# Sample requests in a decode step: 32-row key scores in turns, and values as the moving operand with a product that picks the heads

## The chip, the cores and the metric

The kernel runs on one core of a Trainium2 chip. The metric is device time in microseconds (us): the kernel before takes 3451.75 us, the median of three runs (3449.54 to 3457.61). Engines are named as in the profile: PE does the matmuls, PEld its weight loads, DVE, ACT and POOL the elementwise work, SP issues transfers.

## The reference, cut to what matters

The program is one layer of a hybrid model, for a prompt of 256 tokens and for 8 sample requests of 4 new tokens each. Two of its branches read caches for the sample requests:

```
def diff_attention(q, k, v, ...):          # 8 heads, two key maps each of 64 columns; 256 cached + 4 new keys
    s = einsum('bqhd,bkhd->bhqk', q, k) * 64**-0.5 + bias          # masked where the key is later
    p = softmax(s);  a = p[:, :, 0] - lam * p[:, :, 1]             # map 0 minus lambda times map 1
    o = einsum('bhqk,bkhe->bqhe', a, v)                            # head width 128
def mem_attention(q, mk, mv):              # 4 heads of 128, 256 memory tokens
    p = softmax(einsum('bqhd,bkhd->bhqk', q, mk) * 128**-0.5)
    o = einsum('bhqk,bkhd->bqhd', p, mv)
```

Everything is float32. After the branches come up-projections, an output projection and a large key-retrieval layer (PEER), which the change does not touch.

## The kernel before

The layer runs in stages, each an explicit block in which every engine has its own program, held together by semaphores. At a block's end the engines meet. The order of the work is the order in which it is written; there is no scheduler. The stages that matter are `diff_sample` and `mem_sample`, each after its prompt counterpart, and `diff_norm` behind them.

Beside the attention stages runs a second stream, `GateStream`: the gate columns of the input projection, cut into ticks. A tick is 24 fp32r matmuls on PE (L974, L975, L977), with splits of the weights on ACT (L916) and POOL (L960), a load on SP (L909) and, every fourth tick, an eviction on ACT (L922). Each attention stage calls `gates.pe(pe, n)` between its own steps, so that PE has n ticks of work while the other engines do softmax or evictions. `TICKS_DIFF_SAMPLE = (3, 3)` and `TICKS_MEM_SAMPLE = (4, 2)` are the ticks ahead of the turn of the probabilities and ahead of the value product.

**diff_sample** goes over 4 pairs of requests. `scores(i)`, for each of the two requests s of a pair: 16 transposes turn the keys (L1410), ACT (L1319) and DVE (L1354) copy them out of four banks, then for each of 8 heads a 256-column matmul against the cached keys (L1421) and a 32-column one against the new keys (L1422) add into 64 rows of bank 4 (8 heads, 2 maps, 4 tokens). The stationary operand is a block of queries that is zero outside its own head's rows, so the 8 heads accumulate into one group of rows. `attend(i)`: three ticks, three transposes of the probabilities, three ticks, then the values: for each request, head and page the values are the stationary operand (128x128) and the probabilities move, 4 columns (L1442, 32 matmuls); 8 more matmuls take the new tokens (L1447). ACT evicts the result (L1330) and then takes the exponentials of the next pair (L1324). PE's program is scores(0), scores(1), attend(0), scores(2), attend(1), scores(3), attend(2), attend(3).

**mem_sample** does the same for 2 groups of 4 requests: 8 transposes (L1683), one eviction by ACT of 1024 columns (L1620), and 4 score matmuls into 32 rows (L1691) for each request; values with 32 matmuls of 4 columns (L1709) for each group.

A float32 matmul (other than a transpose) has two records in the trace, each with its own weight load.

Of the kernel before, what the change touches and what calls it, by code (L numbers as in the profile page):

```python
# [252 lines left out]
def decoder_step_kernel(nc, A, O):  # L253
    top = ExitStack()
    with top:
# [20 lines left out]
        with ExitStack() as left, ExitStack() as right:  # L276
# [5 lines left out]
            with ExitStack() as during_attention:  # L282
                x_high, x_low = (tensor(during_attention, "right", f"x_{part}", [P, KT, T], F32R) for part in ("high", "low"))
                input_projections(nc, G, Z, x_high, x_low)
                signals.restart(130)
                attention(nc, G, Z, ODM, x_high, x_low)
# [25 lines left out]
def constants(const):  # L312
# [59 lines left out]
    C["map_is_0_1"] = const("c_map_is_0_1", np.stack([rm == 0, rm == 1], 1))  # L372
    C["iota"] = const("c_iota", np.broadcast_to(np.arange(P), (P, P)))
# [877 lines left out]
def diff_sample(nc, G, Z, OD, v_new, bias_new, bias_own, row_weights, KP, VP, gates):  # L1251
# [4 lines left out]
    PS, ident, A = (G[k] for k in ("PS", "ident", "A"))  # L1256
    ROWS = DIFF_HEADS * 2 * DEC_SEQ
    FT = DIFF_HEADS
    with ExitStack() as ctx:
# [3 lines left out]
        QB = st.sb("q_blocks", [P, 2, FT * (ROWS + 8)])  # L1263
        S, E, PN = (st.sb(w, [P, PAST + NEW]) for w in ("scores", "exps", "probs"))
        AT, ATN = st.sb("a_T", [P, 2, ROWS]), st.sb("a_T_new", [NEW, ROWS])
        mx, nmx, sums, rec, coef = (st.sb(w, [P, 1]) for w in ("max", "neg_max", "sums", "reciprocal", "coefficient"))
        (pages_loaded, zeroed, k_turned, kT_act, kT_dve, q_ready, scores_done, biased, soft, exps, probs, p_turned,
         aT_ready, o_done, o_ready) = st.sems(
            "pages_loaded", "zeroed", "k_turned", "kT_act", "kT_dve", "q_ready", "scores_done", "biased", "soft", "exps",
            "probs", "p_turned", "aT_ready", "o_done", "o_ready")  # L1270
# [12 lines left out]
        with nc.Block() as block:  # L1283
            @block.sync
            def _(sp):
                sp.dma_start(pages[:], A["page_table"].rearrange("(o b) g -> o (b g)", o=1)).then_inc(pages_loaded, 16)
                sp.wait_ge(pages_loaded, after(16))
# [25 lines left out]
            def _(act):  # L1313
                def turn_keys(i):
                    for s in range(2):
                        act.wait_ge(scores_done, after(i * 2 + s))
# [4 lines left out]
                def attend(i, more=True):  # L1321
# [3 lines left out]
                    if more:  # L1325
# [4 lines left out]
                    act.activation(OD[:, 0:FT, ds(i * 8 + SEQ, 8)].rearrange("p h (b s) -> p h b s", b=2),  # L1330
                                   PS[:, 5, 384:384 + ROWS].rearrange("p (b h s) -> p h b s", b=2, s=DEC_SEQ), ACT.Copy).then_inc(o_ready, 1)
# [11 lines left out]
            def _(dve):  # L1343
                def queries_and_keys(i):
                    for s in range(2):
                        dve.wait_ge(scores_done, after(i * 2 + s))
# [9 lines left out]
                def attend(i, more=True):  # L1356
                    dve.wait_ge(scores_done, after(i * 2 + 2))
# [23 lines left out]
                    dve.wait_ge(aT_ready, after(i * 4 + 1))  # L1381
                    dve.tensor_tensor(at, at, turned[:, :, :, 1, :], ALU.add).then_inc(aT_ready, 1)
                    turned = PS[0:NEW, 5, 2 * P:3 * P].rearrange("p (x m s) -> p x m s", m=2, s=DEC_SEQ)
                    at = ATN[:].rearrange("p (x s) -> p x s", s=DEC_SEQ)
                    dve.tensor_copy(at, turned[:, :, 0, :]).then_inc(aT_ready, 1)
                    dve.wait_ge(aT_ready, after(i * 4 + 3))
                    dve.tensor_tensor(at, at, turned[:, :, 1, :], ALU.add).then_inc(aT_ready, 1)
# [6 lines left out]
                attend(DEC_BATCH // 2 - 1, False)  # L1394

            @block.tensor
            def _(pe):
                def scores(i):
                    for s in range(2):
# [14 lines left out]
                        pe.wait_ge(q_ready, after(i * 4 + 2 * s + 2))  # L1414
                        pe.wait_ge(kT_act, after(i * 4 + 2 * s + 2))
                        pe.wait_ge(kT_dve, after(i * 4 + 2 * s + 2))
                        pe.wait_ge(biased, after(i * 2))
                        rows = slice(s * ROWS, (s + 1) * ROWS)
                        for f in range(FT):
                            q = QB[:, s, f * ROWS:(f + 1) * ROWS]  # L1420
                            pe.matmul(PS[rows, 4, 0:PAST], q, KTT[:, s, f, :], start=(f == 0), stop=(f == FT - 1), skip_group_check=True)  # L1421
                            last = pe.matmul(PS[rows, 4, PAST:PAST + NEW], q, Z[:, DK + f, SEQ:T], start=False, stop=(f == FT - 1),  # L1422
                                             skip_group_check=True)
                        last.then_inc(scores_done, 1)

                def attend(i):
                    gates.pe(pe, TICKS_DIFF_SAMPLE[0])
                    pe.wait_ge(probs, after(i + 1))
                    pe.wait_ge(aT_ready, after(i * 4))
# [3 lines left out]
                    gates.pe(pe, TICKS_DIFF_SAMPLE[1])  # L1433
                    pe.wait_ge(aT_ready, after(i * 4 + 4))
                    pe.wait_ge(o_ready, after(i))
                    for s in range(2):
                        pe.wait_ge(v_loaded[s], after(i * 32 + 32))
                        for h in range(FT):
                            c = slice(s * ROWS // 2 + h * DEC_SEQ, s * ROWS // 2 + (h + 1) * DEC_SEQ)
                            out = PS[:, 5, 384 + c.start:384 + c.stop]  # L1440
                            for g in range(N_PAGES):
                                pe.matmul(out, VP[:, s, g, h * P:(h + 1) * P], AT[:, g, c], start=(s == 0 and h == 0 and g == 0),  # L1442
                                          stop=False, skip_group_check=True)
                    for h in range(FT):
                        out = PS[:, 5, 384:384 + ROWS].rearrange("p (b c) -> p b c", b=2)[:, :, h * DEC_SEQ:(h + 1) * DEC_SEQ]
                        new = ATN[:].rearrange("p (b c) -> p b c", b=2)[:, :, h * DEC_SEQ:(h + 1) * DEC_SEQ]
# [1388 lines left out]
```

## Time and profile before

| | |
|---|---|
| median of 3 runs | 3451.75 us (3449.54 to 3457.61) |
| the profiled execution, span | 3452.9 us; the profile gives no other time for it |
| mean granted TensorE clock | 0.940 |
| `diff_sample`, from PE's first transpose to its last matmul | 1019.97 to 1226.24 us |
| `mem_sample`, the same | 1332.97 to 1425.49 us |
| `diff_norm`, PE's part | 1427.25 to 1433.94 us |

How to read it: times in rows count from the span's start. A row of the timeline is a run of like instructions with its start, its length from first start to last end (the last end is modelled), and in brackets the idle time ahead of it with what ended it. PEclk is the granted clock, 1.00 for 2.4 GHz and 0.50 for 1.2 GHz; in between, a stretch held both. PE's records overlap, so the mean duration of one is longer than its share of the time; lengths of runs, and distances between starts, are what counts.

### The profile page before, as it was taken

To read this page: it belongs to the slowest core of one execution; us is meant where nothing else is said; L and a number is where in the kernel's file an instruction comes from. 1 tells how busy PE (TensorE), PEld (TensorE's weight loads), DVE (VectorE), ACT (ScalarE), POOL (GpSimd) and SP (SyncE) were. 2 spreads that over 40 slices of the span, in tenths; PEclk is the share of its full clock that TensorE was granted. 3 is DMA by queue.
4 is the path that set the end of the run, shared out by engine and by line. 5 is a ranking of instruction groups with operands and counts; after the bars stand their busy time and mean duration, and the time that the engine had idled before them with its cause. 6 is when DMAs were issued, how large, how long until landed. Compare 5 with 4: busy or idle time off the path is not lost. (4 is left out here: it accounts for less than half of the span.)

```text
span 3452.9 us, 52978 instructions
## 1 busy us (share of the span) xinstructions
PE 3186.9 (92%) x21228; PEld 2960.5 (86%) x21228; DVE 1822.6 (53%) x2518; ACT 1254.8 (36%) x1374; POOL 1016.1 (29%) x551
## 2 busy tenths in 40 slices
PE   7999997995879978589989999999999999999998
PEld 6999997774878976589989999999999888888886
DVE  5344443332221000246454889987888467777664
ACT  5323232112432223344332444345555333333332
POOL 0000000002543334200240788887777401111000
PEclk9999998666999879789989999999999999999999
DMA  6554453224454453166676778999999978888764
GB/s 211 174 168 157 161 170 117 88 91 142 143 174 152 133 175 114 42 201 209 205 170 123 200 190 243 230 253 285 279 274 275 347 276 294 318 299 312 288 232 158
DMA packets 446570, 696.71 MB, mean 202 GB/s; under 512 B 30205, under 2 KB 342813, under 8 KB 418878
## 3 DMA queue, kind: packets, MB, share of 16 engines
q1 hardware_dynamic: 397086, 554.35, 51.4%
q10 hardware_dynamic: 40128, 73.42, 7.6%
q0 software_dynamic: 9216, 67.11, 5.1%
q8 instruction: 83, 1.36, 0.2%
q14 instruction: 57, 0.47, 0.0%
HBM read 627.94 MB, written 63.70 MB: 200 GB/s over the span
## 5 line engine op out<-in xcount | busy, mean ns | idle before, releaser
L2455 POOL TENSOR_TENSOR peer_uT_low<-peer_uT,peer_uT_high 128x1024 fp32r<-128x1024 f32 x256 | 615.3, 2427 | 262.1 <-ACT peer_uT_high L2482 261.6
L960 POOL TENSOR_TENSOR gate_low<-gate_raw,gate_high 128x512 fp32r<-128x512 f32 x192 | 244.7, 1299 | 1169.0 <-ACT gate_high L916 1168.9
L2355 PE MATMUL banks<-x_high,peer_uT_high 128*128 128x256 f32 x2048 | 495.5, 284 | 8.8 <-ACT peer_picks_T L2514 7.8
L2356 PE MATMUL banks<-x_low,peer_uT_high 128*128 128x256 f32 x2048 | 490.9, 281 | 0.0
L2355 PEld LDWEIGHTS banks<-x_high,peer_uT_high 128*128 128x128 f32 x2048 | 388.1, 189 | 10.0 <-ACT peer_uT_high L2482 7.0
L2356 PEld LDWEIGHTS banks<-x_low,peer_uT_high 128*128 128x128 f32 x2048 | 387.3, 189 | 0.0
L228 PE MATMUL banks<-x_high,win_high 128*128 128x288 f32 (+1 forms) x1312 | 349.1, 296 | 0.0
L229 PE MATMUL banks<-x_low,win_high 128*128 128x288 f32 (+1 forms) x1312 | 348.7, 295 | 0.0
L2482 ACT ACTIVATE peer_uT_high<-peer_uT 128x1024 fp32r<-128x1024 f32 x256 | 261.5, 1054 | 97.0 <-DVE peer_uT L2605 96.0
L198 ACT ACTIVATE win_high<-win_raw 128x2048 fp32r<-128x2048 f32 x84 | 160.8, 1915 | 334.5 <-DVEq L191 329.2
L2605 DVE STREAM_TRANSPOSE peer_uT<-peer_u 128x1024 f32<-128x1024 f32 x192 | 234.4, 1230 | 81.7 <-DMA peer_u<-in_peer_u_dram 53.2
L2362 PE MATMUL banks<-x_high,peer_uT_low 128*128 128x256 f32 x2048 | 263.8, 282 | 0.0
L204 DVE TENSOR_TENSOR win_low<-win_raw,win_high 128x2048 fp32r<-128x2048 f32 x84 | 192.4, 2291 | 115.8 <-ACT win_high L198 115.8
L2362 PEld LDWEIGHTS banks<-x_high,peer_uT_low 128*128 128x128 f32 x2048 | 250.1, 189 | 0.0
L974 PE MATMUL banks<-x_high,gate_high 128*128 128x288 f32 x768 | 222.6, 311 | 29.1 <-ACT gate_out L922 25.1
L229 PEld LDWEIGHTS banks<-x_low,win_high 128*128 128x128 f32 x1312 | 247.2, 188 | 0.0
L228 PEld LDWEIGHTS banks<-x_high,win_high 128*128 128x128 f32 x1312 | 246.5, 188 | 0.2
L975 PE MATMUL banks<-x_low,gate_high 128*128 128x288 f32 x768 | 217.7, 303 | 0.0
L2422 PE MATMUL banks<-x_high 128*128 128x512 f32 x512 | 201.6, 394 | 12.5 <-DVE x_low L2762 12.5
L2530 ACT ACTIVATE peer_uT_high<-peer_u 128x2048 fp32r<-128x2048 f32 x64 | 122.8, 1919 | 228.6 <-PE banks L2424 201.8
L2530 ACT ACTIVATE x_high<-peer_area 128x2048 fp32r<-128x2048 f32 x64 | 122.7, 1919 | 220.2 <-PE banks L2424 218.1
L2463 POOL DMA_INDIRECT peer_area<-in_peer_v_dram,peer_expert_row x32 | 62.0, 1936 | 473.7 <-DVE peer_area L2730 472.6
(390 smaller groups left out, 6884.3 us busy)
## 6 DMA issues: line engine op xcount, KB each, us to landing
win_raw<-in_w_in_dram SPq DMA_DIRECT2D x38, 2048.0 KB, 8.1
peer_u<-in_peer_v_dram SPq DMA_DIRECT2D x64, 1024.0 KB, 6.4
peer_area<-in_peer_v_dram SPq DMA_DIRECT2D x64, 1024.0 KB, 5.0
gate_raw<-in_w_in_dram SPq DMA_DIRECT2D x96, 512.0 KB, 4.0
peer_u<-in_peer_u_dram SPq DMA_DIRECT2D x192, 256.0 KB
peer_u<-in_peer_u_dram ACTq DMA_DIRECT2D x192, 256.0 KB
w_raw<-in_w_up_ret_dram SPq DMA_DIRECT2D x8, 2048.0 KB, 9.6
w_raw<-in_w_out_dram SPq DMA_DIRECT2D x8, 2048.0 KB, 8.8
```

Source lines behind the costliest of these rows:

```text
L228: pe.matmul(out, w, xh[:, k, :], start=(k == 0), stop=False)
L229: pe.matmul(out, w, xl[:, k, :], start=False, stop=False)
L960: pool.tensor_tensor(self.low[:, p % 2, c, :, :], self.raw[:, p % 4, :, c * P:(c + 1) * P], self.high[:, p % 2, c, :, :], ALU.subtract).th ...
L974: pe.matmul(out, high, self.xh[:, 4 * q + k, :], start=(q == 0 and k == 0), stop=False)
L975: pe.matmul(out, high, self.xl[:, 4 * q + k, :], start=False, stop=False)
L2355: pe.matmul(out, UH[:, c, k, :], XH[:, k, 0:DENSE], start=(k == 0), stop=False)
L2356: pe.matmul(out, UH[:, c, k, :], XL[:, k, 0:DENSE], start=False, stop=False)
L2362: last = pe.matmul(out, UL[:, c, k, :], XH[:, k, 0:DENSE], start=False, stop=(k == KT - 1))
L2455: pool.tensor_tensor(UL[:, m % 2, part, :], UT[:, m % 2, part, :], UH[:, m % 2, part, :], ALU.subtract).then_inc(low, 1)
L2482: act.activation(UH[:, m % 2, part, :], UT[:, m % 2, part, :], ACT.Copy).then_inc(uT_high, 1)
L2530: act.activation(VH[n % 4], V[n % 4], ACT.Copy).then_inc(v_high, 1)
L2605: dve.transpose(UT[:, m % 2, b * HALF:(b + 1) * HALF, :].rearrange("p c (E e) -> p E c e", E=4), u_block(m)[:, :, cols].rearrange("p E (c ...
```

## The change

In `diff_sample` a row group is now 32 rows instead of 64: request s and half of the heads (4 heads, 2 maps, 4 tokens). Both requests' keys are turned first, in one go of 32 transposes. Then four rounds follow; in each, one 256-column matmul for each of the four row groups, then one 32-column matmul for each. The number of score matmuls is as before (16 and 16 for a pair); a stationary operand has 32 columns instead of 64.

For the values the operands change places: 32 columns of the turned probabilities (all heads of one request, one page) are stationary, and the values move, 512 columns at a time, into banks 0 and 1. That is 8 matmuls for a pair, and the four combinations of request and page go to the four row groups. Their result holds all products of probabilities of any head with values of any head. ACT and DVE copy it to `ds_values`, and 8 matmuls with a constant 0/1 matrix `pick` keep what belongs together, sum over the two pages, and turn it: values stationary, 8 columns moving. Of the six ticks, one now stands between the value product and this pick. The new tokens' products are left for the end of the stage, 8 matmuls of 32 columns, added by one DVE instruction. The semaphore signals go from 130 to 140, and two small constants are loaded.

`mem_sample` has the same two edits: transposes of two requests, then their scores in turns; 8 value matmuls of 512 columns over four row groups, accumulating over the two halves of the tokens in one bank, an ACT copy, and 4 pick matmuls of 16 columns.

```diff
-                        rows = slice(s * ROWS, (s + 1) * ROWS)
-                        for f in range(FT):
-                            q = QB[:, s, f * ROWS:(f + 1) * ROWS]
-                            pe.matmul(PS[rows, 4, 0:PAST], q, KTT[:, s, f, :], start=(f == 0), stop=(f == FT - 1), skip_group_check=True)
-                            last = pe.matmul(PS[rows, 4, PAST:PAST + NEW], q, Z[:, DK + f, SEQ:T], start=False, stop=(f == FT - 1),
...
+                    tiles = [(s, half, slice((2 * s + half) * TILE, (2 * s + half + 1) * TILE)) for s in range(2) for half in range(2)]
+                    for r in range(FT // 2):
...
+                        for s, half, rows in tiles:
+                            pe.matmul(PS[rows, 4, 0:PAST], queries(s, half), KTT[:, s, half * (FT // 2) + r, :], start=(r == 0),
...
+                        for s, half, rows in tiles:
+                            last = pe.matmul(PS[rows, 4, PAST:PAST + NEW], queries(s, half), Z[:, DK + half * (FT // 2) + r, SEQ:T],
...
-                    gates.pe(pe, TICKS_DIFF_SAMPLE[1])
-                    pe.wait_ge(aT_ready, after(i * 4 + 4))
+                    gates.pe(pe, TICKS_DIFF_SAMPLE[1] - 1)
+                    pe.wait_ge(aT_ready, after(i * 6 + 2))
...
+                    for w in range(2):
+                        for s in range(2):
                             for g in range(N_PAGES):
-                                pe.matmul(out, VP[:, s, g, h * P:(h + 1) * P], AT[:, g, c], start=(s == 0 and h == 0 and g == 0),
...
+                                j = N_PAGES * s + g
+                                last = pe.matmul(PS[32 * j:32 * j + 32, w, :], AT[:, g, s * ROWS // 2:(s + 1) * ROWS // 2],
+                                                 VP[:, s, g, w * 512:(w + 1) * 512], start=True, stop=True, skip_group_check=True)
+                    last.then_inc(o_done, 1)
+                    gates.pe(pe, 1)
...
+                    pe.wait_ge(values_act, after(i + 1))
+                    pe.wait_ge(values_dve, after(i + 1))
...
                     for h in range(FT):
...
+                        last = pe.matmul(PS[:, 5, 384 + h * 8:384 + h * 8 + 8], O[:, h * P:(h + 1) * P], pick[:, h, :],
+                                         start=True, stop=True, skip_group_check=True)
+                    last.then_inc(picked, 1)
```

On PE, in `diff_sample`, the turn and the scores of the first pair before. `ident` is the identity of the transposes, `ds_k_T` the turned keys, `Z` (L1410) the loaded keys and (L1422) the new ones; the left-out rows alternate in the same way:

```order
L1410 MATMUL banks<-ident,Z 128x128 x16
L1421 MATMUL banks<-ds_k_T,ds_q_blocks 64x256
L1422 MATMUL banks<-Z,ds_q_blocks 64x32
...
L1422 MATMUL banks<-Z,ds_q_blocks 64x32
L1410 MATMUL banks<-ident,Z 128x128 x16
L1421 MATMUL banks<-ds_k_T,ds_q_blocks 64x256
L1422 MATMUL banks<-Z,ds_q_blocks 64x32
```

and after, at the same place:

```order
L1431 MATMUL banks<-ident,Z 128x128 x32
L1446 MATMUL banks<-ds_k_T,ds_q_blocks 32x256 x4
L1449 MATMUL banks<-Z,ds_q_blocks 32x32 x4
L1446 MATMUL banks<-ds_k_T,ds_q_blocks 32x256 x4
L1449 MATMUL banks<-Z,ds_q_blocks 32x32 x4
```

The second request's transposes have moved ahead of the first's scores, and the scores of both stand in one block, four row groups in turn.

On PE, the end of `attend(0)` before; the last gate matmuls, the values of both requests, the new tokens' values and the next pair's transposes:

```order
L977 MATMUL banks<-x_high,gate_low 128x288 x4
L1442 MATMUL banks<-ds_a_T,Z 128x4 [waits signal_179,signal_176,signal_174]
L1442 MATMUL banks<-ds_a_T,Z 128x4 x15
L1442 MATMUL banks<-ds_a_T,Z 128x4 [waits signal_180]
L1442 MATMUL banks<-ds_a_T,Z 128x4 x15
L1447 MATMUL banks<-ds_a_T_new,Z 128x2x4 x8
L1410 MATMUL banks<-ident,Z 128x128 [waits signal_165,signal_177]
```

and after:

```order
L985 MATMUL banks<-x_high,gate_low 128x288 x4
L1469 MATMUL banks<-Z,ds_a_T 32x512 [waits signal_185,signal_184,signal_174]
L1469 MATMUL banks<-Z,ds_a_T 32x512 x7
L982 MATMUL banks<-x_high,gate_high 128x288 [waits signal_132]
...
L985 MATMUL banks<-x_high,gate_low 128x288 x4
L1479 MATMUL banks<-ds_pick,ds_values 128x8 [waits signal_179,signal_174,signal_178,signal_177]
```

The 32 matmuls of 4 columns have become 8 of 512, a tick (signal_132 is its split weights) has moved in behind them, and 8 pick matmuls follow it; the new tokens' 8 are gone from here.

## Rows read from the trace of the kernel before

**Rows 1.** The page: the granted clock in 40 slices of the span.
```profile
PEclk9999998666999879789989999999999999999999
```

**Rows 2.** Windows over the stages: us, busy by engine, PEclk, DMA share, GB/s.
```profile
1019.90:1226.70 206.80, 194.60 (x1292) 179.93 (x1292) 23.82 (x74) 45.36 (x88) 61.18 (x48) 0.85 0.43 144
...
1332.90:1365.40 32.50, 23.44 (x128) 13.23 (x128) 2.41 (x13) 10.28 (x14) 0.67 (x1) 1.00 0.07 20
```

**Rows 3.** Timeline of PE, 1062 to 1092: values, new tokens, keys turned.
```profile
1073.43 9.98 PE L1442 MATMUL banks<-ds_a_T,Z 128*128 128x4 f32 x64
1083.35 3.58 PE L1447 MATMUL banks<-ds_a_T_new,Z 32*128 32x8 f32 x16
1086.86 3.67 PE L1410 MATMUL banks<-ident,Z 128*128 128x128 f32 x16
1091.52 0.62 PE L1421 MATMUL banks<-ds_k_T,ds_q_blocks 128*64 128x256 f32 x2 [0.99 <-DVE ds_k_T L1354]
```

**Rows 4.** Windows over the four value blocks, the first and the sum.
```profile
1073.40:1086.90 13.50, 13.50 (x83) 13.46 (x81) 0.00 (x0) 0.00 (x0) 0.00 (x0) 0.65 0.01 3
...
sum 54.50, PE 54.44 PEld 54.20 DVE 0.00 ACT 0.02 POOL 0.00; mean PE 13.61 PEld 13.55 DVE 0.00 ACT 0.01 POOL 0.00
```

**Rows 5.** Windows over the turns and scores: pair 2, and the sum of four.
```profile
1086.86:1103.42 16.56, 14.59 (x98) 11.39 (x97) 4.07 (x11) 4.16 (x9) 2.49 (x2) 0.87 0.53 174
...
sum 68.21, PE 58.55 PEld 45.10 DVE 16.37 ACT 15.68 POOL 7.48; mean PE 19.52 PEld 15.03 DVE 5.46 ACT 5.23 POOL 2.49
```

**Rows 6.** Timeline, 1019 to 1037: both turns of the first pair, softmax of it.
```profile
1019.97 3.34 PE L1410 MATMUL banks<-ident,Z 128*128 128x128 f32 x16 [9.27 <-DMA Z<-in_cache_diff_k_dram]
...
1028.77 1.97 PE L1410 MATMUL banks<-ident,Z 128*128 128x128 f32 x16
...
1036.39 0.42 DVE L1359 TENSOR_TENSOR ds_scores<-banks,diff_bias_new 128x256 f32<-128x256 f32 x1 [4.93 <-PE banks L1422]
...
1038.97 0.38 DVE L1349 TENSOR_SCALAR ds_q_blocks<-Z 64x32 f32<-64x32 f32 x2
1039.38 1.29 DVE L1354 COPY ds_k_T<-banks 128x512 f32<-128x512 f32 x2
...
1040.92 0.62 PE L1421 MATMUL banks<-ds_k_T,ds_q_blocks 128*64 128x256 f32 x2 [2.67 <-DVE ds_k_T L1354]
```

**Rows 7.** Timeline of PE, 1332 to 1350: `mem_sample`'s turns and scores.
```profile
1332.97 1.06 PE L1683 MATMUL banks<-ident,Z 128*128 128x128 f32 x8 [0.94 <-PEq L1479]
1335.15 1.91 PE L1691 MATMUL banks<-msm_k_T,msm_q_blocks 128*32 128x256 f32 x8 [1.11 <-ACT msm_k_T L1620]
1336.99 1.09 PE L1683 MATMUL banks<-ident,Z 128*128 128x128 f32 x8
```

**Rows 8.** Groups by line and form, 1332.9 to 1434: busy, mean ns of one.
```profile
L1691 PE MATMUL banks<-msm_k_T,msm_q_blocks 128*32 128x256 f32 x64 | 15.3, 382 | 9.0 <-ACT msm_k_T L1620 9.0
...
L1691 PEld LDWEIGHTS banks<-msm_k_T,msm_q_blocks 128*32 128x32 f32 x64 | 6.4, 109 | 16.0 <-ACT msm_k_T L1620 10.9
```

**Rows 9.** Timeline of PE, 1384 to 1434: `mem_sample`'s values, `diff_norm`.
```profile
1386.29 8.92 PE L1709 MATMUL banks<-msm_probs_T,memory_cache_v 128*128 128x4 f32 x64
...
1416.78 8.71 PE L1709 MATMUL banks<-msm_probs_T,Z 128*128 128x4 f32 x64
1427.25 6.69 PE L1755 MATMUL banks<-dn_squares,ones 128*128 128x288 f32 x16 [1.76 <-ACT dn_squares L1741]
```

**Rows 10.** Timeline of PE, 854.9 to 857.2: matmuls over 64 input rows, two halves.
```profile
855.29 1.14 PE L1222 MATMUL banks<-dp_qkv_T 64*128 64x256 f32 x8
```

**Rows 11.** Windows over three ticks at either clock, and over the ticks behind L1709.
```profile
1052.80:1062.60 9.80, 9.80 (x75) 9.78 (x73) 0.00 (x0) 3.16 (x5) 5.74 (x5) 1.00 0.44 133
1189.10:1201.70 12.60, 12.10 (x75) 11.86 (x75) 0.69 (x3) 5.54 (x13) 8.13 (x7) 0.83 0.86 295
...
1395.20:1410.40 15.20, 14.70 (x100) 14.46 (x99) 0.52 (x2) 6.11 (x13) 10.14 (x8) 0.90 0.17 54
```

**Rows 12.** The transfers, 1100 to 1140: busy share in 40 slices of 1 us.
```profile
DMA  0059200000799998999999970000000000000039
```

More of the change, by code:

```diff
@@ L1444, in attend @@
+                    last.then_inc(o_done, 1)
+                    gates.pe(pe, 1)
+                    if i == 0:
+                        pe.wait_ge(pick_loaded, after(16))
+                    pe.wait_ge(values_act, after(i + 1))
+                    pe.wait_ge(values_dve, after(i + 1))
+                    pe.wait_ge(aT_ready, after(i * 6 + 6))
                     for h in range(FT):
[L1445 removed]
@@ L1446, in attend @@
-                        new = ATN[:].rearrange("p (b c) -> p b c", b=2)[:, :, h * DEC_SEQ:(h + 1) * DEC_SEQ]
-                        last = pe.matmul(out, v_new[:, h * P:(h + 1) * P], new, start=False, stop=True, skip_group_check=True)
-                    last.then_inc(o_done, 1)
+                        last = pe.matmul(PS[:, 5, 384 + h * 8:384 + h * 8 + 8], O[:, h * P:(h + 1) * P], pick[:, h, :],
+                                         start=True, stop=True, skip_group_check=True)
+                    last.then_inc(picked, 1)
@@ L1454, in _ @@
                 attend(DEC_BATCH // 2 - 1)
+                for h in range(FT):
+                    last = pe.matmul(PS[:, 4, h * NEW:(h + 1) * NEW], v_new[:, h * P:(h + 1) * P], ATN[:, h, :],
+                                     start=(h == 0), stop=True, skip_group_check=True)
+                last.then_inc(new_done, 1)
 GROUP = 4
@@ L1603, in _ @@
             def _(sp):
+                sp.dma_start(pick[:], C["pick_mem"]).then_inc(pick_loaded, 16)
                 gates.sp(sp, TICKS_MEM_SAMPLE[0])
@@ L1689, in scores @@
                             pe.wait_ge(exps, after(i))
                         for f in range(FT):
-                            last = pe.matmul(PS[b * ROWS:(b + 1) * ROWS, 4, 0:MEM_TOKENS], QB[:, b % 2, f * ROWS:(f + 1) * ROWS],
-                                             KTT[:, b % 2, f, :], start=(f == 0), stop=(f == FT - 1))
-                        last.then_inc(scores_done, 1)
+                            for b in (2 * pair, 2 * pair + 1):
+                                last = pe.matmul(PS[b * ROWS:(b + 1) * ROWS, 4, 0:MEM_TOKENS], QB[:, b % 2, f * ROWS:(f + 1) * ROWS],
+                                                 KTT[:, b % 2, f, :], start=(f == 0), stop=(f == FT - 1), skip_group_check=True)
@@ L1695, in attend @@
+                        last.then_inc(scores_done, 2)
                 def attend(i):
@@ L1698, in attend @@
                     pe.wait_ge(pT_ready, after(i))
+                    pe.wait_ge(o_ready, after(i))
                     for k in range(2):
```

139 lines of the change are left out of this document (86 added, 53 removed).

## The prediction

> **What bounds the kernel now.** I read the granted clock by slices first [rows 1]. The reader is to see that the clock is down in slices 8 to 11 (an earlier stage) and again, at 7 to 8 tenths, in single slices up to 19, each of 86 us, where the attention stages lie, and not in the last half. The windows over the two sample stages come next [rows 2]: in `diff_sample` PE is busy for 194.6 of 206.8 us, at a mean clock of 0.85, while DVE has 23.8 us, ACT 45.4 and POOL 61.2. So PE alone sets the time there, and what PE saves the program saves, as long as nobody is late for it. In `mem_sample`'s score part PE is busy for 23.4 of 32.5 us, and waits for an eviction the rest of the time.
>
> Then the timeline of PE. A value block is 64 records in 9.98 us, the new tokens 16 in 3.58, and the next keys' turn takes 3.67 for 16 transposes [rows 3], where the same 16 take 1.97 elsewhere [rows 6]: the clock is down. The windows over the value blocks say so: the first holds 80 records in 13.5 us at a clock of 0.65, and all four come to 54.5 us [rows 4]. In full-clock time that first block is 13.5 x 0.65 = 8.8 us, or 0.11 us a record. Each block begins at the full clock after ticks and ends at half of it; matmuls of 4 and 8 columns are what PE does before it falls. The turns and scores of the four pairs take 68.2 us [rows 5], with one wait of about 1 us for the last DVE copy at each turn [rows 3] and 2.67 us at pair 1, where the softmax of pair 0 stands ahead of the copies [rows 6]. In `mem_sample` a request is 1.06 us of turning, 1.11 us of wait and eight records in 1.84 us (1335.15 to 1336.99) [rows 7], that is 0.23 us for a record of 256 columns in a 32-column group.
>
> **What the score edit costs and gives.** The number of matmuls stays. A block of one request is (1036.3 - 1028.8 - 2.0 - 1.0) / 8 = 0.57 us a head [rows 3, 6], of which two records of 256 columns are 0.46 and the 32-column ones 0.11. If the four row groups run side by side, a round costs PE what one matmul of each kind costs: 0.57 us, so 2.4 us a pair with the filling, where it was 8.8 to 9.0. If they run one after another, a pair stays at 16 x 0.57 = 9.1.
>
> No row of before has two 32-column groups side by side. What I have is the nearest thing, two halves of the array by input rows [rows 10]: eight records of 256 columns in 1.14 us, last end included, so about 1.0 us, where eight records in one group take 1.84 us [rows 7]. They overlap twofold, although the program gives both matmuls of the first half before those of the second. PE thus starts work for a free part of the array past matmuls that wait for a busy one. I take the row groups as fully side by side, and keep one after another as the other end.
>
> The Trainium skill, TensorEngine Tiling (Array Packing), Key Properties, says that different tiles can load weights and multiply in parallel; with the speedup of 3.07 that TensorE: Matmul & The Clock Gate, Measured speedup vs the span model, gives for four tiles by rows, the fourfold terms would be 1.3 times as long, and my sum some 5 us less. That page also has a rule against this change (The mechanism: weight loads overlap running matmuls only where the row group differs, and all tiles here have the same rows). By it the gain of the turns would go, which is my serial rival below. The trace does not bear it out within one group: in the 128x32 matmuls a weight load of 0.109 us stands between records that are 0.23 us apart.
>
> The waits: both turns now come first. Pair 0: 3.3 us of transposes at half clock, 2.0 for the second request, then DVE's last copy, 0.9, then 2.4: 8.6 us. Pair 1: the scores started 4.63 us after the last ones (1036.29 to 1040.92), and behind the softmax DVE now has two sets of query blocks and copies (0.38 and 1.29) [rows 6] where it had one: 6.4 us, and 2.4. Pairs 2 and 3: the same chain without the 1.2 us of bias and maximum, which DVE does during the tick behind the value product: 5.2 and 2.4. Together 8.6 + 8.8 + 7.6 + 7.6 = 32.6 us against 68.2: **35.6 us** less. ACT's exponential still waits for the end of the pair's last product, so the copies can't start earlier; this is what becomes late next.
>
> **The value edit.** Eight matmuls of 512 columns: a record of twice 256 columns is 2 x 0.23 = 0.46, less the fixed part, 0.44 us. Side by side, two rounds of two records are 1.76 us a pair; one after another 7.0. The pick is 16 records at 0.11: 1.8 us. The copies to `ds_values` (512 columns, 0.60 on ACT by its key copy, 0.65 on DVE, half of two in 1.29 [rows 6]) lie beside the tick that was moved behind the product, 3.27 us (9.8 for three [rows 11]); without that cover they would cost 0.8 us a pair. The tick itself is moved, not added; its loads are issued as before, since SP runs up to four ticks ahead. DVE's extra instructions for the new tokens, two of some 0.2 us, lie beside a tick too. At the end come 16 records for the new tokens, 1.8 us, and one DVE addition, with its wait 0.6 us. Sum: 4 x 3.56 + 2.4 = 16.6 us against 54.5 [rows 4]: **37.9 us** less. About half of it is the clock: 320 records at 0.11 would be 35 us.
>
> Behind the third block three ticks took 12.6 us at a clock of 0.83, against 9.8 at 1.00 [rows 11]. I expect the clock to stay up now, as it did in `mem_sample`'s scores, where turns and waits alternate with 256-column matmuls at 1.00 [rows 2, 7]: **2.8 us** less.
>
> **mem_sample and diff_norm.** Two requests are turned (2.1 us), ACT's second eviction of 1.02 us ends 1.3 us later, and eight matmuls in two groups take 1.9: 5.3 us for two, against 8.1. With 0.4 us for the exponential ahead of group 1's copies: 32.5 - 4 x 5.3 - 0.4 = **10.9 us** less. Values: 8.8 and 8.7 us [rows 9] become 1.76 + 0.9 each: **12.2** less. The four ticks behind the first block, 15.2 us [rows 11], become 13.1: **2.1** less. `diff_norm`'s 16 records took 6.69 us at low clock [rows 9]; at 0.26 us each they are 4.2: **2.5** less.
>
> **Small costs.** The array changes its grouping some 12 times more, at 0.1 us each by the excess of a first record: 1.2 us. Ten more signals, 0.2. The two constants are loaded beside the page table and the first ticks.
>
> **Sum:** 35.6 + 37.9 + 2.8 + 10.9 + 12.2 + 2.1 + 2.5 - 1.4 = 102.6 us less than the profiled execution's span of 3452.9, so 3350.3. The median of the runs is 1.1 us under that span, so I say 3350. Later stages do not depend on when they start.
>
> **Rivals.**
> 1. *Half of the overlap* (3370 us): PE keeps strictly to the program's order, so that the second record of a matmul waits for its first and only neighbours overlap, or the four moving operands share a read path, each being 128 rows deep where the halves of [rows 10] read every row once. A 256-column matmul then costs 0.23 in the scores (4.7 us a pair), a 512-column one 0.44: 9 + 7 + 3.5 = 20 us more. For it: nothing in before reads four streams. Against it: the order in [rows 10].
> 2. *No overlap* (3417 us): scores of 9.1 and values of 7.0 a pair in `diff_sample`, 3.7 and 7.0 in `mem_sample`: 27 + 21 + 7.5 + 10.5 = 66 us more. It would still be 1.0% faster, by fewer waits and by the clock.
> 3. *Slower, 3471 us*: each change of row group empties the array and leaves the weight load uncovered. There are 32 changes a pair in the scores, 8 in the values, 48 in `mem_sample`, 208 in all. The price by a record's latency of 0.38 against its spacing of 0.23, plus a load of 0.11 [rows 7, 8], is 0.26 us, so 54 us on top of rival 2. It turns slower from 0.17 us a change. Against it: the change between the halves in [rows 10] cost nothing.
> 4. *The gain is there, but PE waits or slows* (3366 us): keys arrive late, or the clock falls between pick and scores, where 1.8 us of 8-column matmuls are followed by 5 us of transposes and a wait. SP issues the keys of pair 3 ahead of three gate loads; these transfers start at about 1110, 7 us after `attend(1)` began at 1103.42 [rows 5], and keep the engines busy until 1124 [rows 12]. The whole of `attend` shrinks to 23.8 us (six ticks 19.6, turn 0.6, values and pick 3.6), so a margin of 3 us stays. If the clock falls at three or four turns, each costs 3 to 4 us.
>
> **Chances.** Full overlap 0.55; half of it 0.20; waits or clock 0.08; none 0.13; slower 0.04. The time is that of the first. A range from 3338 to 3405 holds the first, second and fourth with their errors and leaves out most of the two serial ones. A change under 0.2%, 7 us, can't be told from none: faster 0.95, same 0.01, slower 0.04.
>
> **What would show it.** Timeline of PE: a round of four 256-column matmuls about 0.5 us long, four row groups' records starting within some tens of ns; a score block of 2.4 us, a value block of 1.8, a pick of 1.8 at full clock; the wait ahead of the scores 1.3 us in pairs 2 and 3; the clock over `diff_sample` at 0.95 or more, and the stage some 130 us long. I am wrong if a score block is over 4.5 us, if the clock still falls in each pair, or if idle time ahead of a tick grows over 2 us.

## The result and the profile after

| | before | after | predicted |
|---|---|---|---|
| median | 3454.68 us (4 runs, 3449.54 to 3458.73) | 3352.91 us (4 runs, 3349.06 to 3357.17) | 3350 (3338 to 3405) |
| ratio | | 0.9708, 95% interval 0.9691 to 0.9726 | 0.9705 |
| span of the profiled execution | 3452.9 us | 3353.8 us | 3350.3 |
| mean granted clock | 0.940 | 0.947 | |
| PE in `diff_sample`, first transpose to last matmul | 206.3 us | 133.0 us | 130.0 |
| PE in `mem_sample`, the same | 92.5 us | 68.2 us | 67.3 |

The change is faster by 2.9%. Of the 99.1 us between the two spans, 73.3 lie in `diff_sample` and 24.3 in `mem_sample`; the stages between are 1.4 us shorter, `diff_sample` starts 0.8 us earlier, and from `diff_norm` on nothing is gained. (The predicted stage lengths are those of before less the terms of the sum, without its 1.4 us of small costs.)

The page after, granted clock by slices, answers [rows 1]:

```profile
PEclk9999999666999899799989999999999999999999
```

With 84 us a slice, `diff_sample` lies in slices 13 and 14 now (9 and 8 tenths) and `mem_sample` in slice 16 (9); what is left below lies in other stages. The 8 of slice 14 comes from behind the stage: the clock was 1.00 from 1090.0 to the stage's end at 1152.2 us, and 0.50 in the 22 us after it. The windows over `diff_sample`, over `mem_sample`'s turns and scores, and over the ticks behind its first values (us, busy by engine, PEclk, DMA share, GB/s) answer [rows 2, 11]:

```profile
1019.10:1152.40 133.30, 122.27 (x1116) 111.08 (x1116) 27.25 (x87) 47.84 (x92) 61.20 (x48) 0.99 0.67 224
...
1257.40:1277.50 20.10, 15.32 (x129) 10.38 (x129) 2.21 (x13) 9.85 (x14) 0.79 (x1) 1.00 0.12 36
...
1301.00:1314.90 13.90, 13.40 (x100) 13.16 (x100) 0.52 (x2) 6.12 (x13) 10.09 (x8) 1.00 0.20 63
```

The clock over `diff_sample` rose from 0.85 to 0.99. PE's idle time did not go: 11.0 of 133.3 us, where it was 12.2 of 206.8. What went is work of PE and the slow clock.

The timeline of PE from `attend(0)`'s values to pair 2's scores answers [rows 3 to 5]:

```profile
1055.81 1.92 PE L1469 MATMUL banks<-Z,ds_a_T 128*32 128x512 f32 x16
...
1060.97 1.85 PE L1479 MATMUL banks<-ds_pick,ds_values 128*128 128x8 f32 x16
1062.67 2.38 PE L1431 MATMUL banks<-ident,Z 128*128 128x128 f32 x20
1065.45 1.53 PE L1431 MATMUL banks<-ident,Z 128*128 128x128 f32 x12 [0.40 <-DVE ds_k_T L1369]
1067.98 0.64 PE L1446 MATMUL banks<-ds_k_T,ds_q_blocks 128*32 128x256 f32 x8 [1.00 <-DVE ds_k_T L1369]
1068.41 0.24 PE L1449 MATMUL banks<-Z,ds_q_blocks 128*32 128x32 f32 x5
...
1068.51 0.61 PE L1446 MATMUL banks<-ds_k_T,ds_q_blocks 128*32 128x256 f32 x7
...
1069.90 0.27 PE L1449 MATMUL banks<-Z,ds_q_blocks 128*32 128x32 f32 x8
```

Values and pick are 1.92 and 1.85 us for the 13.5 of before. The turn of 32 transposes starts at the full clock and takes 4.31 us with one wait for an eviction. A round of scores is 8 records of 256 columns and 8 of 32, each round begins 0.5 us after the last, and the block ends 2.19 us after it began (1067.98 to 1070.17). From the end of the pick to the scores' end are 7.4 us where [rows 5] has 16.56.

Pair 1's turn, and the groups of the score and value lines over the stage (busy, mean ns of one, idle before):

```profile
1031.05 1.97 PE L1431 MATMUL banks<-ident,Z 128*128 128x128 f32 x16 [3.49 <-DMA Z<-in_cache_diff_k_dram]
1033.45 1.97 PE L1431 MATMUL banks<-ident,Z 128*128 128x128 f32 x16 [0.44 <-DMA Z<-in_cache_diff_k_dram]
```

```profile
L1446 PE MATMUL banks<-ds_k_T,ds_q_blocks 128*32 128x256 f32 x128 | 8.5, 382 | 4.0 <-DVE ds_k_T L1369 4.0
L1469 PE MATMUL banks<-Z,ds_a_T 128*32 128x512 f32 x64 | 7.7, 598 | 0.0
L1479 PE MATMUL banks<-ds_pick,ds_values 128*128 128x8 f32 x64 | 7.4, 251 | 0.0
```

The keys of pair 1 are now late: PE waits 3.9 us for them. And a trap for readers: one score record still lasts 382 ns, as in [rows 8], though 128 of them fill 8.5 us (66 ns each). Records in different row groups overlap, so the mean duration tells nothing of the throughput.

`mem_sample` after, the first turn and scores, the end of the stage, and ACT's last steps, answer [rows 7, 9]:

```profile
1257.47 1.94 PE L1727 MATMUL banks<-ident,Z 128*128 128x128 f32 x16 [1.05 <-PEq L1516]
1260.56 1.92 PE L1736 MATMUL banks<-msm_k_T,msm_q_blocks 128*32 128x256 f32 x16 [1.16 <-ACT msm_k_T L1661]
1262.41 1.97 PE L1727 MATMUL banks<-ident,Z 128*128 128x128 f32 x16
...
1318.29 1.92 PE L1753 MATMUL banks<-Z,msm_probs_T 128*32 128x512 f32 x16
1324.57 1.06 PE L1761 MATMUL banks<-msm_pick,msm_values 128*128 128x16 f32 x8 [0.99 <-ACT msm_values L1676]
1327.92 6.61 PE L1806 MATMUL banks<-dn_squares,ones 128*128 128x288 f32 x16 [2.28 <-ACT dn_squares L1792]
```

```profile
1322.02 0.41 ACT L930 ACTIVATE gate_out<-banks 128x288 f32<-128x288 f32 x1 [5.37 <-PE banks L985]
1323.62 0.41 ACT L930 ACTIVATE gate_out<-banks 128x288 f32<-128x288 f32 x1 [1.19 <-PE banks L985]
1323.93 0.59 ACT L1676 ACTIVATE msm_values<-banks 128x512 f32<-128x512 f32 x1
```

The last copy of the products is not hidden: ACT's program has the eviction of the last gate tile ahead of it, and that waits for the very tick behind the value product (1323.62), so the copy starts when the tick is over. And `diff_norm` is as long as before.

### The profile page after: what moved, and what is told of

The parts are those of the page before. It is cut to its first block and busy times, and to the rows that moved or that the text cites. A ratio compares the mean times of both kernels' runs of the same rounds, so it can differ in the third digit from the quotient of the medians.

```text
span 3353.8 us, 52494 instructions
## 1 busy us (share of the span) xinstructions
PE 3095.2 (92%) x20972; PEld 2873.7 (86%) x20972; DVE 1820.4 (54%) x2531; ACT 1257.0 (37%) x1380; POOL 1016.0 (30%) x551
## 5 line engine op out<-in xcount | busy, mean ns | idle before, releaser
L2533 ACT ACTIVATE peer_uT_high<-peer_uT 128x1024 fp32r<-128x1024 f32 x256 | 260.5, 1055 | 63.3 <-DVE peer_uT L2656 62.6
```

Source lines behind the costliest of these rows:

```text
L2533: act.activation(UH[:, m % 2, part, :], UT[:, m % 2, part, :], ACT.Copy).then_inc(uT_high, 1)
```

## The experiments

All ratios are against the kernel before in the same job. Because executions scatter by some 5 us and `diff_sample` starts up to 10 us apart in them, PE's own time in the two stages (first transpose to last matmul) is the sharper measure; the ratio has the last word where a version as a whole is judged.

| | median us | ratio, 95% | `diff_sample` | `mem_sample` |
|---|---|---|---|---|
| before | | 1 | 206.3 | 92.5 |
| the change | 3352.91 | 0.9708 (0.9691 to 0.9726) | 133.0 | 68.2 |
| 1 scores of `diff_sample` alone | 3422.12 | 0.9908 (0.9873 to 0.9942) | 179.1 | 98.1 |
| 2 values of `diff_sample` alone | 3412.15 | 0.9873 (0.9851 to 0.9894) | 167.0 | 95.7 |
| 3 `mem_sample` alone | 3426.41 | 0.9921 (0.9903 to 0.9939) | 206.8 | 68.1 |
| 4 before, ticks among the values | 3440.39 | 0.9958 (0.9943 to 0.9972) | 197.0 | 92.5 |
| 5 change, group by group | 3374.52 | 0.9769 (0.9747 to 0.9791) | 149.0 | 71.7 |
| 6 change, two groups of 64 rows | 3358.59 | 0.9722 (0.9701 to 0.9743) | 140.3 | 68.2 |
| 7 change, pair 1's keys first | 3354.65 | 0.9701 (0.9682 to 0.9720) | 132.4 | 68.2 |
| 8 as 7, ticks behind the turns | 3346.19 | 0.9688 (0.9670 to 0.9705) | 132.1 | 61.3 |
| 9 change, two rounds a group | 3363.10 | 0.9732 (0.9712 to 0.9752) | 142.2 | 68.2 |
| 10 the change again, with 9 and 11 | 3352.73 | 0.9697 (0.9678 to 0.9715) | 134.2 | 68.2 |
| 11 as 8 again | 3343.51 | 0.9681 (0.9666 to 0.9696) | 131.6 | 62.6 |

**1 to 3: one part alone.** The first takes the new `scores` and keeps the old `attend`, the second the other way round, the third has the old `diff_sample` and the new `mem_sample`.

> The kernel before with only the score edit of diff_sample (both requests turned first, four 32-row groups in turns); values, mem_sample and all else as before. Theory (row groups run side by side, so a pair's scores take 2.2 us instead of 8.8): the turns and scores of the four pairs go from 68.2 to about 37 us (34.2 in the changed kernel, plus about 3 because the old value blocks still leave a low clock to the turns behind them), so 31 us less, ratio about 0.991. Rival (much of the gain of the changed kernel came from the clock and the waits, and the scores are a small part): under 15 us less, ratio above 0.9955.

> The kernel before with only the value edit of diff_sample (values moving, pick, new tokens at the end); scores by 64 rows as before, mem_sample as before. Theory: the value blocks go from 54.5 to 17 us, the clock stays up, so the third group of ticks loses its 2.8 us and the score blocks of pairs 2 and 3 their 5.8 us at low clock: 46 us less, ratio about 0.987. Rival (the clock was held up in the changed kernel by the short turns and scores, not by the value edit): the clock falls behind the pick, 36 us less, ratio 0.9895.

> The changed kernel with diff_sample as before; mem_sample changed. Theory (the parts add up): mem_sample takes 68.1 us instead of 92.5, 24 us less, ratio about 0.993, and e1, e2 and e3 together give the 99 us of the changed kernel within 3. Rival (the parts lean on each other by clock or transfers): the three differ from 99 us by more than 8.

Measured: spans 31.5, 40.5 and 30.5 us shorter, and 27.2, 39.3 and 24.4 us less in the stage that was changed. In the first, the score block is the same 2.19 us, and the values keep their price, here `attend(1)`'s:

```profile
1101.91 11.43 PE L1449 MATMUL banks<-ds_a_T,Z 128*128 128x4 f32 x64
```

and the group of that line over the stage:

```profile
L1449 PE MATMUL banks<-ds_a_T,Z 128*128 128x4 f32 x256 | 44.1, 311 | 0.0
```

Its values come to 44.1 us, more than before (9.98 [rows 3], 9.23, 9.89 and 11.31 make 40.4): the clock falls earlier in the last three blocks, and the mean clock of the stage is 0.82. The two `diff_sample` edits alone give 66.5 us, together 73.3. Of the 6.8 between, 3.7 are the slower value blocks of the first. Some 4 lie in the second, ahead of its first value block, where its code is still that of before: the clock there was 0.83 for 0.96, and two score blocks took 6.88 and 5.96 us for 4.54. The slow turns of the first (5.9 us each, 4.3 with both edits) add only 1.2, for before has slow turns too (3.67 [rows 3]), and a score block that met the slow clock before (6.77 us, in pair 2) and does so in neither of the two takes 2.2 back. So what looks like an interplay of the edits is mostly where the slow clock fell. By the ratios the parts add up: 0.92 + 1.27 + 0.79 = 2.98% against 2.92%. The `mem_sample` of 1 and 2 is longer than before although its code is the same: its two value blocks are 11.7 and 11.2 us in 1, at a mean clock of 0.59 and 0.62, where they are 8.92 and 8.71 [rows 9] at 0.79 and 0.81. A block of these sparse matmuls costs more or less by how much of it meets the slow clock.

**4: how much of the value edit is the clock.** Nothing is changed but the place of three ticks in the kernel before: one ahead, one between the two requests' values, one ahead of the new tokens.

```
-                    gates.pe(pe, TICKS_DIFF_SAMPLE[1])
+                    gates.pe(pe, 1)
                     for s in range(2):
+                        if s:
+                            gates.pe(pe, 1)
...
+                    gates.pe(pe, 1)
                     for h in range(FT):
```

> The kernel before with one edit: in diff_sample's attend, two of the three ticks ahead of the values stand among them (one between the two requests' values, one ahead of the new tokens' values); same instructions, same count. Theory (PE's clock falls because the 80 records of 4 and 8 columns stand in one stretch): the clock stays up, the value records cost 0.11 us each, 35 us instead of 54.5, the ticks lose 2.8 and the score blocks 5.8 of low clock: up to 28 us less, ratio 0.992. Rival (half stretches of 3.5 us of such matmuls are enough to bring it down, or it falls for another reason): no change, ratio 0.998 to 1.002.

The timeline of PE over `attend(0)` and the next turn, and the group of the values over the stage:

```profile
1062.39 3.63 PE L1444 MATMUL banks<-ds_a_T,Z 128*128 128x4 f32 x32
1070.67 3.87 PE L1444 MATMUL banks<-ds_a_T,Z 128*128 128x4 f32 x32
1079.08 1.95 PE L1450 MATMUL banks<-ds_a_T_new,Z 32*128 32x8 f32 x16
1080.96 1.97 PE L1410 MATMUL banks<-ident,Z 128*128 128x128 f32 x16
```

```profile
L1444 PE MATMUL banks<-ds_a_T,Z 128*128 128x4 f32 x256 | 32.2, 262 | 0.0
```

The values fell from 40.4 to 32.2 us, the new tokens from 3.58 to 1.95 each, the turn from 3.67 to 1.97. But the clock still fell, and the ticks between took it: seven of the eight took 4.7 to 6.0 us, where a tick is 3.27 [rows 11], 12.7 us more in all. The mean clock of the stage is 0.90. The span is 17.3 us shorter, the median 13.6, the stage 9.3; only the last is surely this edit's, since 3.6 us of the span lie ahead of the stage and the rest behind it. The mean clock over the stage in [rows 2], 0.85, says that the slow clock had cost 0.15 x 206.8 = 31 us of it, so less than a third came back, between the two expectations. Eight half blocks at the full clock would be 8 x 3.5 = 28 us, and with 4 x 1.95 for the new tokens 36. So by this estimate the value edit's 37.9 us are about 18 of clock (54.5 less 36) and 20 of records that are no longer issued.

**5, 6 and 9: what the overlap hangs on.** The same matmuls on the same row groups, in another order: all of a group's, then the next group's (5, in both stages, scores and values); the two rounds of a group, then the next group's (9, scores of `diff_sample`). 6 has two groups of 64 rows in turn, with twice the rounds.

```
                     for s, half, rows in tiles:
+                        for r in range(FT // 2):
...
-                    for w in range(2):
-                        for s in range(2):
-                            for g in range(N_PAGES):
+                    for s in range(2):
+                        for g in range(N_PAGES):
+                            for w in range(2):
```

> The changed kernel with the same matmuls in another order: each row group's score matmuls stand together (group 0's eight, then group 1's), and each row group's value matmuls too, in diff_sample and mem_sample. Theory A (PE starts work for a free row group past matmuls that wait for a busy one, as far as it is asked to): a score block of a pair stays at 2.2 to 3 us, a value block at 1.9. Theory B (it looks only a few instructions ahead, so turns in the written order are needed): value blocks, with 4 records a group, stay near 1.9 to 2.5, but score blocks, with 16 records a group, go to 6 to 9 us: 16 to 26 us more than the changed kernel. Theory C (strict order): value blocks 5.4 us and score blocks 8.5, 45 us more.

> The changed kernel, but diff_sample's scores in two groups of 64 rows in turns (one request each, 8 rounds) instead of four of 32. Theory (side by side, so a block takes as long as one group's list of matmuls): 8 rounds at 0.5 to 0.57 us, 4.0 to 4.6 us a pair instead of 2.2, 8 to 10 us more over four pairs. Rival (what counts is that both requests are issued together, and half the width is as good): under 2 us more.

> The changed kernel with one other order of diff_sample's score matmuls: two rounds of one row group (4 matmuls, 8 records) in a row, then the next group's two rounds, and so twice over the four groups. With group by group (16 records in a row) the block took 6.67 us, against 9.1 serial: each of the 3 changes of group gave back about 0.8 us, some four to six records. Theory B (PE looks only a few records ahead of a waiting one): here there are 7 changes; each gives back 0.6 to 0.8 us, so a block takes 9.1 - 7 x 0.6 to 0.8 = 3.5 to 4.9 us, 1.3 to 2.7 more than the changed kernel's 2.19, 5 to 11 us more in all: 3358 to 3364. Theory C (the look-ahead is a share of the group, or covers 8 records): the block stays at 2.2 to 2.5 us and the time within 2 us of 3353. Theory D (a change to a group that has been used before costs more, whatever the number of records): 6 us or more a block.

The timeline of PE in 5, from the first group's first to the second group's second round:

```profile
1024.45 0.59 PE L1446 MATMUL banks<-ds_k_T,ds_q_blocks 128*32 128x256 f32 x2 [0.99 <-DVE ds_k_T L1369]
1024.88 0.22 PE L1448 MATMUL banks<-Z,ds_q_blocks 128*32 128x32 f32 x2
...
1025.43 0.60 PE L1446 MATMUL banks<-ds_k_T,ds_q_blocks 128*32 128x256 f32 x2
1025.86 0.22 PE L1448 MATMUL banks<-Z,ds_q_blocks 128*32 128x32 f32 x2
1025.92 0.62 PE L1446 MATMUL banks<-ds_k_T,ds_q_blocks 128*32 128x256 f32 x4
1026.36 0.25 PE L1448 MATMUL banks<-Z,ds_q_blocks 128*32 128x32 f32 x4
1026.45 0.60 PE L1446 MATMUL banks<-ds_k_T,ds_q_blocks 128*32 128x256 f32 x2
```

Read the counts: rows of x2 are one group alone, rows of x4 are two groups at once. Only the last round of a group, four records, runs beside the first of the next. So 16 rounds take the time of 13, 6.67 us a block. In 9, the same view:

```profile
1028.63 0.59 PE L1447 MATMUL banks<-ds_k_T,ds_q_blocks 128*32 128x256 f32 x2 [0.99 <-DVE ds_k_T L1369]
1029.06 0.22 PE L1449 MATMUL banks<-Z,ds_q_blocks 128*32 128x32 f32 x2
1029.12 0.62 PE L1447 MATMUL banks<-ds_k_T,ds_q_blocks 128*32 128x256 f32 x4
1029.55 0.25 PE L1449 MATMUL banks<-Z,ds_q_blocks 128*32 128x32 f32 x4
1029.64 0.62 PE L1447 MATMUL banks<-ds_k_T,ds_q_blocks 128*32 128x256 f32 x4
```

7 changes of group, each with one round of overlap, leave the time of 9 rounds: rounds start 0.52 apart, and a block takes 4.79 us, inside theory B's 3.5 to 4.9, and the stage is 9.2 us longer. C and D fall. The groups of the lines in 5, scores and values of `diff_sample` and scores of `mem_sample`:

```profile
L1446 PE MATMUL banks<-ds_k_T,ds_q_blocks 128*32 128x256 f32 x128 | 26.4, 382 | 4.0 <-DVE ds_k_T L1369 4.0
L1468 PE MATMUL banks<-Z,ds_a_T 128*32 128x512 f32 x64 | 7.8, 598 | 0.0
L1735 PE MATMUL banks<-msm_k_T,msm_q_blocks 128*32 128x256 f32 x64 | 11.2, 382 | 4.7 <-ACT msm_k_T L1660 4.7
```

The values don't mind the order, 7.8 us for 7.7: a group has only four records there, and all four groups still run at once: the first four records of the block start within 0.15 us, the fourth past twelve records that the program has first, nine of them still waiting. The scores of `mem_sample`, 8 records a group, keep the overlap of four: 2.81 us a pair, where 8 + 8 - 4 records at 0.23 are 2.76. All three sizes fit one account: each row group can hold about four records, one at work and the rest waiting, and PE moves on until a record finds its group full. That is an account of these runs; no run counted the places directly, by five or six records a group.

In 6 the block is 4.58 us, eight rounds of 0.55: twice the rounds of half as many groups, 2.0 times overlap for the four groups' fourfold. Its stage is 7.3 us longer, where 4 x 2.4 = 9.6 were at stake; pair 1's keys, late in the changed kernel, cost it 1.28 us for 3.93.

**7: the late keys of pair 1.** SP loads the keys of the second pair ahead of the values of the first:

```
-                load_values(0)
                 load_keys(1)
+                load_values(0)
```

> The changed kernel, with SP issuing the keys of pair 1 ahead of the values of pair 0 (which are needed 25 us later). Theory (the 3.49 us wait ahead of pair 1's turn is the keys standing behind 2 MB of values in the transfers): the wait goes to under 1 us, after which DVE's copies behind the softmax decide: 2 to 2.5 us less in the profile, not to be told from none by time. Rival (the keys are late by their own issue and size): the wait stays over 2.5 us.

The timeline of PE, pair 1's turn:

```profile
1036.57 1.97 PE L1431 MATMUL banks<-ident,Z 128*128 128x128 f32 x16 [0.49 <-DMA Z<-in_cache_diff_k_dram]
1039.85 1.97 PE L1431 MATMUL banks<-ident,Z 128*128 128x128 f32 x16 [1.32 <-DMA Z<-in_cache_diff_k_dram]
```

The wait at the start went from 3.49 to 0.49, one of 1.32 came in the middle, and the scores started 6.7 us after the last ones ended, where it was 8.8. But pair 0's turn took 6.63 us where it was 5.22, at a clock of 0.55 for 0.70, and the stage is 132.4 us for 133.0. That the order of the loads brought the clock down is not shown: 8 and 11 have the same order and first turns of 5.29 and 5.44 us. Within the interval it makes no difference.

**8, 10 and 11: ticks in the gaps.** On top of 7, one of the three leading ticks stands between the turn and the scores, in `mem_sample` two of four, and there DVE makes the copy for which PE waited:

```
+                    if i:
+                        gates.pe(pe, 1)
                     pe.wait_ge(q_ready, after(i * 4 + 4))
...
-                    gates.pe(pe, TICKS_DIFF_SAMPLE[0])
+                    gates.pe(pe, TICKS_DIFF_SAMPLE[0] - (i + 1 < DEC_BATCH // 2))
...
+                    dve.wait_ge(o_done, after(i + 1))
+                    dve.wait_ge(picked, after(i))
+                    dve.tensor_copy(O[:], PS[:, 0, :]).then_inc(values_ready, 1)
```

> The changed kernel with the keys of pair 1 first, one tick moved into each gap between a turn and its scores (pairs 1 to 3 in diff_sample, all four in mem_sample, with ACT's ticks moved to match) and mem_sample's copy of the products done by DVE. Theory: the waits of 1.0 to 1.4 us behind the turns (three), 1.16 us (four) and 0.99 ahead of the last pick go: 8 us less than the changed kernel, and 2 more by the keys, so some 3343 to 3345 us. Rival (the copies are late by what ACT now does ahead of them, the wait only moves ahead of the next tick): within 2 us of the changed kernel.

> The changed kernel itself, on the same chip as the version with ticks in the turns, for a direct comparison: 3349 to 3357, ratio 0.970 to 0.972 against the kernel before.

> The version with the keys loaded first, a tick in each gap behind the turns, and DVE copying mem_sample's product, again, on the same chip as the changed kernel: if its 7.5 us by the profiled spans are real, 3345 to 3348, and 5 to 9 us below the changed kernel in the same job; if they were scatter between executions, within 3 us of it.

In one job, 3343.51 us (3342.32 to 3345.50) against 3352.73 (3342.28 to 3358.44), five runs each. The medians are 9.2 us apart (8.5 between 7 and 8, also in one job), but one run of the changed kernel is as fast as the version's fastest, and the intervals of the two ratios overlap: likely some 7 us (0.2%), not certain. The stage times say where: `mem_sample` is 5.6 to 6.9 us shorter, its four waits of 1.16 gone and the 0.99 ahead of the last pick; `diff_sample` only 0.9 to 2.6. There the rival of the expectation is in part right: two of the three ticks behind a turn now open with a wait of 0.85 us for ACT's eviction of a gate tile, where the scores had waited 0.99 and 1.00, so only one of three waits went. At the end of `mem_sample` the gain is partly handed back:

```profile
1315.46 0.96 PE L1766 MATMUL banks<-msm_pick,msm_values 128*128 128x16 f32 x8
1319.96 5.84 PE L1811 MATMUL banks<-dn_squares,ones 128*128 128x288 f32 x16 [3.54 <-ACT dn_squares L1797]
```

`diff_norm`'s matmuls wait 3.54 us for ACT's squares where they waited 2.28.

## Why the prediction was right, point by point

The forecast was 3350 us by full overlap, and it came to 3352.9. Rivals 1 to 3 each fall with the score block of 2.19 us: half of the overlap gave 4.7, none 9.1. But rival 1 named something real. PE does stop at a row group whose places are taken, as 5 and 9 show; the round-robin order of the change, and the four records a group of the values, keep it from mattering. Rival 4 named something real too, in another place: keys arrived late, but pair 1's and not pair 3's, for 3.9 us. Had the loops been written the other way, the two stages would have been 19.5 us longer (16.0 and 3.5).

- *Turns and scores, 35.6 us.* 68.2 [rows 5] became 34.2, so 34.0. The block is 2.19 (predicted 2.4), the wait ahead of the scores 1.00 (1.3). Pairs 2 and 3 take 7.4 each (7.6). The miss is pair 1, 11.0 us where 8.8 stood: its chain was worked out from DVE's bias, maximum and copies, and the keys' transfer behind the first values was not in it. The chain itself was right: in 5, where PE waited for no keys at pair 1, the scores started 6.36 us after those of pair 0 ended (1031.05 to 1037.41; 6.4 predicted). In 7, with 1.8 us of waits for keys left, pair 1 took 8.9 us (1036.0 to 1044.9), 2.1 less than in the changed kernel.
- *Values, 37.9 us.* Block 1.92, pick 1.85, with the new tokens at the end 1.97 and DVE's addition 0.42: as predicted within 1 us. The copies stay beside the tick.
- *Clock behind, 2.8 us.* The ticks behind the third block took 10.5 us where 9.8 stood, at the full clock: 2.1. Three ticks take 9.7 to 10.5 us at full clock, and the upper ones hold a wait of 0.50 us for a gate tile's eviction; a lower one, without it, had been taken.
- *`mem_sample`, 10.9 + 12.2 + 2.1.* Scores 12.5: a pair took 4.97, not 5.3, and the second group's exponential cost next to nothing. Values 11.0: the last copy, 1.0 us, was costed as covered, and the cover was wrong. ACT's own program waits for the tick ahead of it. Ticks 1.5 (13.7 us for 13.1).
- *`diff_norm`, 2.5 us.* This step failed. The matmuls took 6.61 us for 6.69. The term laid their low clock to the sparse matmuls ahead; with these gone the clock was full until PE stood idle for ACT's squares (2.28 us), and then was at half again, as the windows over the last tick with the pick and over `diff_norm`'s matmuls show:

```profile
1314.90:1325.60 10.70, 9.71 (x75) 7.82 (x73) 0.00 (x0) 2.74 (x6) 2.54 (x2) 1.00 0.06 21
1326.30:1333.00 6.70, 5.08 (x11) 3.65 (x12) 0.91 (x2) 3.50 (x3) 0.00 (x0) 0.51 0.01 0
```
  The other versions of the change have the same 16 records in 5.8 to 7.1 us. Whether the idle time alone brings the clock down there, before and after, no run separates. The 0.26 us a record was an estimate for the full clock; no run shows these records at it.
- *Small costs, 1.4 us.* Not separable; nothing in the trace asks for more.
- *Readings.* Counted from 1, the slices of [rows 1] at 6 to 8 tenths are 7 to 10, 14, 15, 17, 18 and 21, not 8 to 11 and up to 19. The difference in the first score estimate is 0.56 us a head, not 0.57, and the rows are 0.55 apart. Pair 1's wait adds up to 6.3, not 6.4. None of it moves the sum by more than 0.3 us.

By stages, predicted and measured savings are: `diff_sample` 75.3 (the three terms less 1.0 of small costs) and 73.3; `mem_sample` 24.8 and 24.3; `diff_norm` with its wait 2.5 and -0.4; the start and the stages between 0 and 2.2; the rest 0 and -0.3. That makes 102.6 and 99.1. The 2.2 us are in no term of the sum, and `diff_sample` starts up to 10 us apart between executions, so that the spans agree this closely is in part luck; the two stages, 97.6 for 100.1, are the fair measure.

Of the rule that speaks against this change in the Trainium skill, TensorE: Matmul & The Clock Gate, The mechanism (weight loads overlap running matmuls only where the row group differs), the runs show the opposite for columns: all four groups read the same 128 rows, and their 256-column records, each with its weight load of 110 ns, start together. In the first 0.2 us of a value block of 5, eight weight loads and four records start, and within a group the 512-column records follow each other by 0.43 us where those of 256 columns do by 0.23 [rows 7], so the load's 0.11 is not in the distance. The speedup is 4.15 for the score block (9.08 to 2.19 us), above the 3.07 that the same page has for four tiles by rows and the 2.38 for three by columns (Measured speedup vs the span model). Both are for 512 columns; at 512 columns the value block here comes to about 3.7, by the prediction's estimate of 7.0 us for one after another against 1.92.

## What to carry to other kernels

Where a float32 stationary operand has 32 columns or fewer of use, four of them side by side cost PE what one costs, as the score and value blocks here do; write the matmuls in turns over the groups, or at most four records of a group in a row, for in the longer runs tried here only the last four overlapped. Where a product has few moving columns, exchange the operands, take the products that nobody wants, and pick afterwards: it saves the issued records and, as much again, the clock that sparse matmuls lose for themselves and for what follows. When the bounding engine gets faster, look at what was in nobody's way: here a transfer queue's order (3.9 us of wait, though setting it right alone did not show in the time), and an eviction that stands ahead of the copy in ACT's own program.

## What the runs showed that was not expected

- Overlap goes by places in each row group, about four records (6.67, 4.79 and 2.81 us in the three orders that put more in a row, 1.94 for 1.92 us where there are four), not by the distance in the program: PE had nine records waiting in three groups and still began the fourth group's.
- The same 64 sparse records took 8.7 to 11.7 us by how much of the block met the slow clock, and which part did changed from version to version (44.1 us for four blocks in 1, 40.4 before). A change elsewhere in the program can move such a block by 2 to 3 us, and in 1 and 2 `mem_sample`, whose code is that of before, was 3 to 6 us longer. The last block of 16 sparse records, behind the pick, met it as well: 1.97 us in the change, 2.52 in the same kernel again (10), 3.10 in 8.
- A tick between sparse blocks got the clock back only in part, and seven of eight such ticks took 4.7 to 6.0 us for 3.27: dense work in between shifts the price as well as saving it.
